# First pair of expert units written out ahead of the loop, its up product before two of the shared expert's down products

## The chip, the core and the metric

The kernel runs on one core of a Trainium2 chip. The metric is device microseconds for one call, the median of several runs. A profiled execution gives one trace beside them. TensorE (PE) does matrix products and transposes, VectorE (DVE) and ScalarE (ACT) do arithmetic and copies, GpSimd (POOL) issues the gathers of token rows, and SyncE (SP) issues nearly all other transfers. All engines run on their own and meet at semaphores.

## What is computed

One layer of a hybrid backbone over 384 tokens (128 of context, 256 latent): token mixers (gated linear attention and latent attention), then a mixture of experts. The part that the change touches is the last:

```python
def moe(h, lp):
    ...
    _, top_e = lax.top_k(jnp.where(e_mask, sel, -jnp.inf), TOP_K)   # 8 of 64 experts for a token
    ...
        a = jax.nn.silu(jnp.einsum('td,edf->tef', tb, lp['w_exp_gate'])) * jnp.einsum('td,edf->tef', tb, lp['w_exp_up'])
        a = a * gb[:, :, None].astype(a.dtype)
        return jnp.einsum('tef,efd->td', a, lp['w_exp_down'])
    ...
    shared = (jax.nn.silu(t @ lp['w_sh_gate']) * (t @ lp['w_sh_up'])) @ lp['w_sh_down']
    return (routed + shared).reshape(b_, l_, d)
```

Model width is 1024, each of the 64 experts has a hidden width of 256, all in float32. The three matrices of an expert are 1.05 MB each, 201 MB for all 64.

## The kernel before, in words

Ahead of the experts the kernel runs the token mixers, the router and the shared expert. The shared expert has three steps for each tile `t` of 128 tokens: `shared_up(t)`, `shared_turn(t)` (transposes of its activations) and `shared_down(t)`, two groups of four matmuls into the PSUM banks 0 and 1 (`hbank`), each taken to `acc` by ACT in `shared_out(t)`.

Experts are then handled in units of two, 128 token slots to a unit, and units in pairs, `half` 0 and 1. A pair `p` on PE (`pair`, L1055) is, in this order: `up(p, 0)`, 64 matmuls of the gathered tokens `xs` with the gate and up weights `raw_gu` of the unit into bank 0; `scatter` of the unit before (its output `ys` times the 0/1 matrix `place`, into banks 4 to 7, added to `acc` by DVE), three of six parts; `turn`, the transposes of the gated activations; the other three parts of the scatter; `gate_slots`, the gates and rows of the next pair's slots; `down(p, 0)`, 32 matmuls with `raw_dn` into banks 1 and 2; then the same for half 1, with `tokens_t`, the transposes of the next pair's gathered tokens, in place of the slots. ACT does `silu`, `take_turned`, `high_y` and half of `tokens`; DVE does `gated`, `add_scattered`, `gate_slots`, `places`, `low_y`, `picks` and the other half of `tokens`. POOL gathers the token rows `xg` of pair p+1 with two indirect DMAs when the slots are there and the old tokens have been transposed.

The weights of a unit are six loads of 1.05 MB, four for `raw_gu[half]`, two for `raw_dn[half]`. There are two sets of buffers, for half 0 and half 1, so the sync queue issues the loads of units 0 and 1 ahead of the loop and those of unit u+2 in a loop: `raw_gu[half]` when `up_done` shows that the up product of unit u is through, then `raw_dn[half]` when `y_done` shows the same for the down product. These waits stand in one queue in the order of the code.

The first pair runs through the same loop as the others (`Fori(0, ...)`). A unit before unit 0 does not exist. Its scatter is done all the same, with zeros: DVE clears `place` (L1822) and `ys` (L1866), and PE multiplies and DVE adds six tiles of zeros in the first pass. All three `shared_down` stand ahead of the loop, two before the tables of the overflow units (`overR`, `overJ`, `overK`), the third after them (L1041). Before its loop each engine loads two numbers of pairs, `n_pairs` and `final`, into registers. In this case there are 16 pairs, 7 of them wide.

Of the kernel before, what the change touches and what calls it, by code (L numbers as in the profile page):

```python
# [12 lines left out]
F32 = mybir.dt.float32  # L13
# [7 lines left out]
P = 128  # L21
D = 1024
NC = D // P
NT = 3
# [13 lines left out]
QPU = P // QTR  # L38
PAIR = 2 * P
# [78 lines left out]
def build(nc, A, O):  # L118

    ctx = ExitStack()  # L120
    with ctx:
# [175 lines left out]
        def rtile(*shape):  # L297
# [6 lines left out]
            if len(shape) == 3:  # L304
# [28 lines left out]
                 "score_ready mask_ready cnt_sb ownm_ready owner_ready jobs_ready tables_ready sh_sil_ready sh_a_ready "  # L333
                 "begun weight_ready h21_taken x1_half sq_half xm_ready h2_out row_ready row_taken xt_done next_ready shared_done zeroed gt2_in scaled_sb high_sb low_sb z_ready y_ready y_out "
                 "pick_ready gtmp_ready xs_act xs_dve gates_done slots_done place_ready up_done silu_done gated "
# [36 lines left out]

        def hbank(n, w=512):
            return ps[:, hr_no[n] % 2, 0:w]

# [146 lines left out]
        def _(pe):  # L522
            def mm(out, l, r, first, last):
                return nc.tensor.matmul(out, l, r, start=first, stop=last)  # L524
# [372 lines left out]

            def gate_slots(first):

                for k in range(2):  # L900
                    for t in range(NT):
                        g = gmov[:, t, first + k, :] if isinstance(first, int) else gmov[:, t, bass.ds(first + k, 1), :].rearrange("p a b -> p (a b)")
                        last = mm(ps[:, 2 if isinstance(first, int) else 3, PAIR + k * GCOL:PAIR + (k + 1) * GCOL], pick[:, t, k * P:(k + 1) * P], g, t == 0, t == NT - 1)
                last.then_inc(S["gates_done"], 1)
# [40 lines left out]
            pe.wait_ge(S["pick_ready"], 1)  # L945
            gate_slots(0)
            shared_turn(1)
            shared_turn(2)
            shared_down(0)
            shared_down(1)  # L950
            pe.wait_ge(S["owner_ready"], 1)
# [88 lines left out]

            shared_down(2)  # L1041
            pe.wait_ge(S["tables_ready"], 1)
            pe.wait_ge(S["wo_sb"], len(wo))
            pe.wait_ge(S["misc_sb"], len(misc))
            pe.sem_inc(S["turned"], 1)
            pe.sem_inc(S["y_done"], 2)
            for half in range(2):
                pe.wait_ge(xg_in[half], 16)
                for n in range(2):
                    tokens_t(half, n)  # L1050
            pe.wait_ge(S["hr_sb"], len(hr))
            n_pairs = pe.value_load(jobs[0:1, NJOB:NJOB + 1], min_val=NMAIN // 2, max_val=NUNIT // 2)
            final = pe.value_load(jobs[0:1, NJOB + 1:NJOB + 2], min_val=NMAIN // 2 - 1, max_val=NUNIT // 2 - 1)
# [22 lines left out]

            with pe.Fori(0, WIDE // 2) as p:
                pair(p, True)
# [25 lines left out]
        def _(act):  # L1104
# [148 lines left out]
            shared_out(0)  # L1253
            shared_out(1)
            shared_out(2)

# [24 lines left out]

            act.wait_ge(S["shared_done"], 1)
            act.sem_inc(S["ast_ready"], 1)
            tokens(0, 0)
            tokens(0, 1)
            n_pairs = act.value_load(jobs[0:1, NJOB:NJOB + 1], min_val=NMAIN // 2, max_val=NUNIT // 2)
            final = act.value_load(jobs[0:1, NJOB + 1:NJOB + 2], min_val=NMAIN // 2 - 1, max_val=NUNIT // 2 - 1)

            with act.Fori(0, final) as p:
                silu(p, 0)  # L1290
                take_turned(p, 0)
                high_y(p, 0)
                silu(p, 1)
                take_turned(p, 1)
                act.wait_ge(S["up_done"], 2 * p + 2)
                tokens(p + 1, 0)
                tokens(p + 1, 1)
                high_y(p, 1)
# [10 lines left out]
        def _(dve):  # L1309
# [462 lines left out]
            def picks(p):  # L1772
                cols_ = posq[:, :, bass.ds(p * 2 * QPU, 2 * QPU)] if not isinstance(p, int) else posq[:, :, 0:2 * QPU]
                V.tensor_tensor(pick[:].rearrange("p t (j s) -> p t j s", s=QTR),
                                slotrow.rearrange("p (j s) -> p j s", s=QTR).unsqueeze(1).to_broadcast([P, NT, 2 * QPU, QTR]),
                                cols_.unsqueeze(3).to_broadcast([P, NT, 2 * QPU, QTR]), ALU.is_equal).then_inc(S["pick_ready"], 1)

            def gate_slots(p):

                dve.wait_ge(S["gates_done"], p + 1)  # L1780
                o = ps[:, 2 if isinstance(p, int) else 3, PAIR:PAIR + 2 * GCOL].rearrange("p (k g) -> p k g", k=2)
                V.tensor_scalar(slot_row[:].unsqueeze(2), o[:, :, 2 * QPU:2 * QPU + 1], -1.0, float(TOK), ALU.mult, ALU.add).then_inc(S["row_ready"], 1)  # L1782
                V.tensor_copy(next_slots[:, 0:2].unsqueeze(2), o[:, :, 2 * QPU:2 * QPU + 1])
                V.tensor_tensor(gtmp, o[:, :, 0:2 * QPU], mine.unsqueeze(1).to_broadcast([P, 2, 2 * QPU]), ALU.mult).then_inc(S["gtmp_ready"], 1)
                dve.wait_ge(S["gtmp_ready"], p + 1)
                V.tensor_reduce(next_slots[:, 2:4], gtmp, AX.X, ALU.add).then_inc(S["next_ready"], 1)

            dve.wait_ge(S["misc_sb"], misc_no["tabK"] + 1)
            picks(0)
            gate_slots(0)  # L1790
            shared_act(2)
# [29 lines left out]

            V.memset(place[:].bitcast(F32), 0.0).then_inc(S["zeroed"], 1)  # L1822

# [5 lines left out]
            def places(k):  # L1829
                V.tensor_scalar(place[:, k, :], token, gtok[:, k:k + 1], None, ALU.is_equal).then_inc(S["place_ready"], 1)  # L1830
# [30 lines left out]
            take_slots(0)  # L1861
            dve.wait_ge(S["zeroed"], 1)
            dve.sem_inc(S["place_ready"], 1)
            places(0)
            dve.wait_ge(S["hr_done"], len(hr))
            V.memset(ys[:].bitcast(F32), 0.0).then_inc(S["zeroed"], 1)  # L1866
            dve.wait_ge(S["zeroed"], 2)
            dve.sem_inc(S["yl_done"], 2)
            dve.wait_ge(S["hr_sb"], len(hr))
            n_pairs = dve.value_load(jobs[0:1, NJOB:NJOB + 1], min_val=NMAIN // 2, max_val=NUNIT // 2)  # L1870
            final = dve.value_load(jobs[0:1, NJOB + 1:NJOB + 2], min_val=NMAIN // 2 - 1, max_val=NUNIT // 2 - 1)
# [25 lines left out]

            with dve.Fori(0, final) as p:
                dve.wait_ge(S["gates_done"], p + 1)
                picks(p + 1)  # L1900
                gated(p, 0)
                add_scattered(p, 0)
                gate_slots(p + 1)
                places(1)
                low_y(p, 0)
                gated(p, 1)
                add_scattered(p, 1)
                dve.wait_ge(S["up_done"], 2 * p + 2)
                tokens(p + 1, 0)
                tokens(p + 1, 1)  # L1910
                take_slots(p + 1)
                places(0)
                low_y(p, 1)
# [106 lines left out]
```

## Time and profile before

| | us |
|---|---|
| median of 3 runs | 791.27 (789.76 to 793.42) |
| the profiled execution | 791.03 |
| its span, from first to last instruction | 789.1 |
| PE busy in it | 746.7 (95%) |
| DVE busy | 392.7 (50%) |
| ACT busy | 133.7 (17%) |

Mean granted clock of TensorE is 0.998 of full speed. The page divides the span into 40 slices of 19.7 us each. The expert units begin at about 283 us, when the first matmul with `raw_gu` runs. The core moved 268.67 MB of data in the span, 340 GB/s on average.

In the rows below, a timeline row reads: start in us, duration in us, engine, line and operation, what it writes and reads, shapes, and how many instructions were merged into the row (such a row's duration runs from the start of the first to the end of the last). Brackets give idle time of the engine ahead of it and what ended that.

### The profile page before, as it was taken

Reading aid. Unit: us, or ns where it says so; the run is one execution under the profiler, and the core shown is the slowest. Engines: PE = TensorE matmul, PEld = TensorE weight load, DVE = VectorE, ACT = ScalarE, POOL = GpSimd, SP = SyncE. Lnnn points to the kernel's source line nnn. Section 1 sums busy time; section 2 is a strip of 40 time slices with the busy share of each in tenths; the row PEclk is TensorE's granted clock in tenths of the full one; section 3 lists DMA queues with packets and bytes.
Section 4 is the critical chain, followed back from the end, with each engine's and each line's share of the span. In section 5 each row is a group of like instructions: output and inputs, shape, how many; then the busy total and the mean of one; then the engine's idle time right before and its main releaser. Section 6 shows DMA issues by size and latency. Waiting matters only on the chain.

```text
span 789.1 us, 13795 instructions
## 1 busy us (share of the span) xinstructions
PE 746.7 (95%) x5071; PEld 361.3 (46%) x5071; DVE 392.7 (50%) x873; ACT 133.7 (17%) x285; POOL 43.1 (5%) x49
## 2 busy tenths in 40 slices
PE   4999998889999999999999999999999999999998
PEld 0554434475555554454454445444544453444433
DVE  2236369483686354364364345443543454435457
ACT  3124001310112112112112011111121111111110
POOL 0000001000000100101101101101011011010100
PEclk9999999999999999999999999999999999999999
DMA  9994466560702999999999999999999999999992
GB/s 339 385 385 144 172 230 233 206 211 1 276 28 81 381 387 422 419 422 419 421 421 420 421 420 420 422 419 420 421 421 421 420 420 421 419 420 422 420 405 85
DMA packets 49911, 268.67 MB, mean 340 GB/s; under 512 B 6300, under 2 KB 8732, under 8 KB 22752
## 3 DMA queue, kind: packets, MB, share of 16 engines
q1 hardware_dynamic: 45280, 255.77, 80.1%
q0 software_dynamic: 4608, 12.59, 4.1%
q8 instruction: 15, 0.25, 0.1%
q14 instruction: 8, 0.07, 0.0%
HBM read 269.01 MB, written 3.52 MB: 345 GB/s over the span
## 4 chain that ended last, share of the span: by engine, by line
PE 54%; DMA 33%; DVE 8%; SPq 2%; issue 2%; ACT 1%; DVEq 0%; ACTq 0%
PE ps L524 50%; DMA raw_gu<-in_w_exp_up 32%; DMA ada<-in_w_ada 1%; PE ps L972 1%; SPq L464 1%; SPq L465 1%; PE ps L831 0%; DVE probT L1537 0%; DVE small L1455 0%; DVE sq L1454 0%; DVE x L1620 0%; PE ps L598 0%; DVE xtmp L1618 0%; DVE h L1644 0%; DVE kend L1484 0%
## 5 line engine op out<-in xcount | busy, mean ns | idle before, releaser
L524 PE MATMUL ps<-raw_gu,xs 128*32 128x512 f32 x2048 | 226.1, 593 | 16.8 <-DMA raw_gu<-in_w_exp_up 15.9
L524 PEld LDWEIGHTS ps<-raw_gu,xs 128*32 128x32 f32 x2048 | 69.1, 110 | 171.5 <-issue 157.0
L524 PE MATMUL ps<-raw_dn,ast 128*32 128x512 f32 x1024 | 116.5, 595 | 0.0
L1856 DVE TENSOR_TENSOR acc<-acc,ps 128x512 f32<-128x512 f32 x186 | 113.6, 678 | 0.0
L1841 DVE SCALAR_TENSOR_TENSOR act_a<-ps,small,sil 128x256 f32<-128x256 f32 x32 | 15.5, 483 | 188.6 <-ACT sil L1261 188.6
L524 PE MATMUL ps<-ys,place 128*128 128x512 f32 x372 | 101.7, 410 | 0.0
L524 PEld LDWEIGHTS ps<-ys,place 128*128 128x128 f32 x372 | 65.4, 189 | 37.0 <-issue 26.0
L1849 DVE TENSOR_TENSOR ys<-ps,ys 128x512 fp32r<-128x512 f32 x60 | 41.5, 692 | 65.2 <-ACT ys L1274 65.2
L524 PEld LDWEIGHTS ps<-raw_dn,ast 128*32 128x32 f32 x1024 | 30.0, 109 | 60.2 <-issue 58.2
L1963 POOL DMA_INDIRECT xg<-h_spill,slot_row x32 | 31.9, 996 | 456.2 <-DVE slot_row L1782 451.3
L1274 ACT CAST ys<-ps 128x512 fp32r<-128x512 f32 x60 | 35.2, 586 | 113.0 <-PE ps L524 113.0
L1261 ACT ACTIVATE sil<-ps 128x256 f32<-128x256 f32 x32 | 12.3, 385 | 219.7 <-PE ps L524 219.7
L524 PE MATMUL ps<-w_out,mixedT 128*128 128x512 f32 x96 | 42.8, 595 | 1.1 <-issue 1.1
L972 PE MATMUL ps<-keep,xg 128*128 128x128 f32 x256 | 36.0, 288 | 0.0
L972 PEld LDWEIGHTS ps<-keep,xg 128*128 128x128 f32 x256 | 33.7, 194 | 3.9 <-issue 0.5
L524 PEld LDWEIGHTS ps<-w_out,mixedT 128*128 128x128 f32 x96 | 17.6, 190 | 20.6 <-issue 20.4
L1834 DVE COPY xs<-ps 128x512 f32<-128x512 f32 x32 | 22.0, 686 | 5.4 <-PE ps L972 5.4
L1279 ACT COPY xs<-ps 128x512 f32<-128x512 f32 x32 | 18.8, 587 | 28.2 <-PE ps L972 28.2
L524 PE MATMUL ps<-ada,small 128*2 128x256 f32 x128 | 11.4, 465 | 11.7 <-DMA ada<-in_w_ada 11.7
L524 PE MATMUL ps<-w_shgu,h2T 128*128 128x512 f32 x48 | 21.8, 598 | 0.0
L524 PE MATMUL ps<-hT,w_qk 128*128 128x384 f32 x64 | 21.8, 491 | 0.0
L524 PE MATMUL ps<-w_g,hT 128*128 128x512 f32 x48 | 21.4, 599 | 0.0
(300 smaller groups left out, 639.0 us busy)
## 6 DMA issues: line engine op xcount, KB each, us to landing
raw_gu<-in_w_exp_gate SPq DMA_DIRECT2D x64, 1024.0 KB, 16.4
raw_gu<-in_w_exp_up SPq DMA_DIRECT2D x64, 1024.0 KB, 18.5
raw_dn<-in_w_exp_down SPq DMA_DIRECT2D x64, 1024.0 KB, 18.7
ada<-in_w_ada SPq DMA_DIRECT2D x16, 512.0 KB, 11.3
ada2a<-in_w_ada SPq DMA_DIRECT2D x8, 1024.0 KB, 5.1
ada2b<-in_w_ada SPq DMA_DIRECT2D x8, 1024.0 KB, 6.3
w_out<-in_w_out SPq DMA_DIRECT2D x1, 4096.0 KB, 12.1
w_qk<-in_w_in SPq DMA_DIRECT2D x2, 1024.0 KB, 13.6
```

Of the source, the lines that this page charges most:

```text
L464: sp.dma_start(raw_gu[half][j][:, 0], gate_of(e)).then_inc(gu_in[half], 16)
L465: sp.dma_start(raw_gu[half][j][:, 1], up_of(e)).then_inc(gu_in[half], 16)
L524: return nc.tensor.matmul(out, l, r, start=first, stop=last)
L972: last = nc.tensor.transpose(ps[:, 4 + 2 * half + n, c * P:(c + 1) * P], xg[:, half, 4 * n + c::NC], ident)
L1261: nc.scalar.activation(sil[:], ps[:, 0, 0:DE], ACT.Silu).then_inc(S["silu_done"], 1)
L1274: nc.scalar.copy(ys[:, 0, n * 512:(n + 1) * 512], ps[:, 1 + n, :]).then_inc(S["yh_done"], 1)
L1279: nc.scalar.copy(xs[:, 0:4, half * P:(half + 1) * P], ps[:, 4 + 2 * half, :].rearrange("p (c s) -> p c s", c=4))\
L1834: V.tensor_copy(xs[:, 4:8, half * P:(half + 1) * P], ps[:, 5 + 2 * half, :].rearrange("p (c s) -> p c s", c=4))\
L1841: V.scalar_tensor_tensor(act_a[:], ps[:, 0, DE:2 * DE], gslot[:, half:half + 1], sil[:], ALU.mult, ALU.mult)\
L1849: V.tensor_tensor(ys[:, 1, h], ps[:, 1 + n, :], ys[:].bitcast(F32)[:, 0, h], ALU.subtract).then_inc(S["yl_done"], 1)
L1856: V.tensor_tensor(a, a, ps[:, 4 + (6 * half + k) % 4, :], ALU.add).then_inc(S["acc_done"], 1)
L1963: G.indirect_dma_start(xg[:, half], None, h2_dram, bass.IndirectOffsetOnAxis(ap=slot_row[:, half:half + 1], axis=0), bounds_check=TOK - 1, ...
```

## The change

The loops of PE, ACT and DVE begin at pair 1, and pair 0 is written out by hand. In it

- the scatter of the missing unit, its additions and both memsets are left out; the semaphores it would have raised are raised by hand;
- `up(0, 0)` comes before `shared_down(1)` and `shared_down(2)`, which take the place of that scatter on PE; their results go to banks 1 and 2, and ACT takes them between `silu(0, 0)`, `take_turned(0, 0)` and `high_y(0, 0)`;
- the tokens' transposes wait for the last overflow table's copy as before, but ACT's copies of them do not wait for the shared results any more;
- the wait for the tables and the loads of the two numbers of pairs come after pair 0.

```diff
         def hbank(n, w=512):
+            if n[0:3] in ("sd1", "sd2"):
+                return ps[:, 1 + int(n[3]), 0:w]
             return ps[:, hr_no[n] % 2, 0:w]
...
             shared_down(0)
-            shared_down(1)
             pe.wait_ge(S["owner_ready"], 1)
...
-            shared_down(2)
-            pe.wait_ge(S["tables_ready"], 1)
             pe.wait_ge(S["wo_sb"], len(wo))
             pe.wait_ge(S["misc_sb"], len(misc))
             pe.sem_inc(S["turned"], 1)
             pe.sem_inc(S["y_done"], 2)
+            pe.sem_inc(S["scat_done"], 6)
             for half in range(2):
                 pe.wait_ge(xg_in[half], 16)
                 for n in range(2):
                     tokens_t(half, n)
+            pe.wait_ge(S["hr_sb"], hr_no["sd01"] + 1)
+            pe.wait_ge(S["next_ready"], 1)
+            up(0, 0, True)
+            shared_down(1)
+            turn(0, 0, True)
+            shared_down(2)
+            pe.wait_ge(S["pick_ready"], 2)
+            pe.wait_ge(S["ast_ready"], 2)
+            gate_slots(2)
             pe.wait_ge(S["hr_sb"], len(hr))
+            down(0, 0, True)
+            up(0, 1, True)
+            scatter(0, 1, range(3))
+            turn(0, 1, True)
+            scatter(0, 1, range(3, 6))
+            for half in range(2):
+                pe.wait_ge(xg_in[half], 32)
+                for n in range(2):
+                    pe.wait_ge(S["acc_done"], 9 + 2 * half + n)
+                    tokens_t(half, n)
+            down(0, 1, True)
+            pe.wait_ge(S["tables_ready"], 1)
             n_pairs = pe.value_load(jobs[0:1, NJOB:NJOB + 1], min_val=NMAIN // 2, max_val=NUNIT // 2)
...
-            with pe.Fori(0, WIDE // 2) as p:
+            with pe.Fori(1, WIDE // 2) as p:
                 pair(p, True)
...
             shared_out(0)
-            shared_out(1)
-            shared_out(2)
...
-            act.wait_ge(S["shared_done"], 1)
             act.sem_inc(S["ast_ready"], 1)
             tokens(0, 0)
             tokens(0, 1)
+            silu(0, 0)
+            shared_out(1)
+            take_turned(0, 0)
+            shared_out(2)
+            high_y(0, 0)
+            silu(0, 1)
+            take_turned(0, 1)
+            act.wait_ge(S["up_done"], 2)
+            tokens(1, 0)
+            tokens(1, 1)
+            high_y(0, 1)
+            act.wait_ge(S["shared_done"], 1)
...
-            V.memset(place[:].bitcast(F32), 0.0).then_inc(S["zeroed"], 1)
...
             take_slots(0)
-            dve.wait_ge(S["zeroed"], 1)
             dve.sem_inc(S["place_ready"], 1)
             places(0)
-            dve.wait_ge(S["hr_done"], len(hr))
-            V.memset(ys[:].bitcast(F32), 0.0).then_inc(S["zeroed"], 1)
-            dve.wait_ge(S["zeroed"], 2)
             dve.sem_inc(S["yl_done"], 2)
+            dve.sem_inc(S["acc_done"], 6)
+            dve.wait_ge(S["gates_done"], 1)
+            picks(1)
+            gated(0, 0)
+            gate_slots(1)
+            places(1)
+            low_y(0, 0)
+            gated(0, 1)
             dve.wait_ge(S["hr_sb"], len(hr))
+            add_scattered(0, 1)
+            dve.wait_ge(S["up_done"], 2)
+            tokens(1, 0)
+            tokens(1, 1)
+            take_slots(1)
+            places(0)
+            low_y(0, 1)
...
-            with dve.Fori(0, final) as p:
+            with dve.Fori(1, final) as p:
```

Queues of SP and POOL are unchanged.

## Rows read from the trace of the kernel before

**Rows 1.** The page: GB/s in 40 slices; the gathers' queue (packets, MB, share).

```profile
GB/s 339 385 385 144 172 230 233 206 211 1 276 28 81 381 387 422 419 422 419 421 421 420 421 420 420 422 419 420 421 421 421 420 420 421 419 420 422 420 405 85
...
q0 software_dynamic: 4608, 12.59, 4.1%
```

**Rows 2.** Stretches: from:to, length, five engines' busy us, granted clock, DMA share, GB/s.

```profile
290.00:291.00 1.00, 1.00 (x5) 0.81 (x6) 0.57 (x2) 0.39 (x1) 0.00 (x0) 1.00 0.20 82
291.00:292.00 1.00, 1.00 (x7) 0.87 (x6) 1.00 (x2) 0.08 (x1) 0.00 (x0) 1.00 1.03 164
292.00:293.00 1.00, 1.00 (x6) 0.81 (x5) 1.00 (x3) 0.29 (x1) 0.00 (x0) 1.00 0.82 344
293.00:424.00 131.00, 131.00 (x1072) 58.95 (x1070) 60.65 (x122) 21.31 (x42) 9.90 (x10) 1.00 1.01 421
```

**Rows 3.** PE's timeline, one row; PE's waits for gate/up loads (total, times, longest).

```profile
434.49 7.07 PE L524 MATMUL ps<-raw_gu,xs 128*32 128x512 f32 x64 [1.55 <-DMA raw_gu<-in_w_exp_up]
...
PE ps L524 <- DMA raw_gu<-in_w_exp_up: 15.9, 22, 1.7
```

**Rows 4.** Timeline of the sync queue: first of four gate/up loads, and down loads.

```profile
290.15 0.33 SPq L464 DMA_DIRECT2D raw_gu<-in_w_exp_gate  x1
...
297.38 0.84 SPq L469 DMA_DIRECT2D raw_dn<-in_w_exp_down  x2
304.40 0.33 SPq L464 DMA_DIRECT2D raw_gu<-in_w_exp_gate  x1
...
320.14 0.34 SPq L464 DMA_DIRECT2D raw_gu<-in_w_exp_gate  x1
```

**Rows 5.** PE's timeline around the first pair.

```profile
267.06 7.03 PE L524 MATMUL ps<-w_shd,sh_aT 128*128 128x512 f32 x16
274.02 0.26 PE L524 MATMUL ps<-rt,late 64*1 64x56 f32 x2
...
276.42 3.70 PE L524 MATMUL ps<-w_shd,sh_aT 128*128 128x512 f32 x8
279.96 1.95 PE L972 MATMUL ps<-keep,xg 128*128 128x128 f32 x16
282.88 7.07 PE L524 MATMUL ps<-raw_gu,xs 128*32 128x512 f32 x64 [0.97 <-ACT xs L1279]
289.88 1.69 PE L524 MATMUL ps<-ys,place 128*128 128x512 f32 x6
...
293.68 3.64 PE L524 MATMUL ps<-raw_dn,ast 128*32 128x512 f32 x32
...
312.89 7.05 PE L524 MATMUL ps<-raw_gu,xs 128*32 128x512 f32 x64
```

**Rows 6.** DVE's timeline: last table, memset of ys, first instruction in the loop.

```profile
277.30 0.51 DVE L1766 TENSOR_TENSOR gmov<-ps,gmov 128x336 fp32r<-128x336 f32 x1
...
283.69 1.76 DVE L1866 MEMSET ys<- 128x2048 f32 x1 [0.37 <-issue]
287.46 0.96 DVE L1774 TENSOR_TENSOR pick<-keep,posq 128x768 fp32r<-128x768 f32 x1 [2.01 <-issue]
```

**Rows 7.** POOL's timeline: two gathers; then the tile's landing times, one each.

```profile
266.86 1.20 POOL L1963 DMA_INDIRECT xg<-h_spill,slot_row  x1 [20.11 <-DVE slot_row L1782]
268.36 0.99 POOL L1963 DMA_INDIRECT xg<-h_spill,slot_row  x1 [0.30 <-issue]
...
DMA to landing us min/median/max: 8.8/8.8/8.8
...
DMA to landing us min/median/max: 10.9/10.9/10.9
```

**Rows 8.** PE's timeline after an idle gap; two stretches, columns as in rows 2.

```profile
134.95 1.06 PE L693 MATMUL ps<-keep,key 128*96 128x128 f32 x4 [2.38 <-DVE keyT L1503]
...
10.50:11.50 1.00, 0.99 (x8) 0.11 (x8) 0.00 (x0) 1.00 (x2) 0.00 (x0) 1.00 1.06 406
...
135.50:138.00 2.50, 2.50 (x14) 2.36 (x13) 2.33 (x5) 0.00 (x0) 0.00 (x0) 0.50 0.47 200
```

More of the change, by code:

```diff
@@ L333, in build @@
                  "score_ready mask_ready cnt_sb ownm_ready owner_ready jobs_ready tables_ready sh_sil_ready sh_a_ready "
-                 "begun weight_ready h21_taken x1_half sq_half xm_ready h2_out row_ready row_taken xt_done next_ready shared_done zeroed gt2_in scaled_sb high_sb low_sb z_ready y_ready y_out "
+                 "begun weight_ready h21_taken x1_half sq_half xm_ready h2_out row_ready row_taken xt_done next_ready shared_done gt2_in scaled_sb high_sb low_sb z_ready y_ready y_out "
                  "pick_ready gtmp_ready xs_act xs_dve gates_done slots_done place_ready up_done silu_done gated "
@@ L896, in _, with gate_slots @@
             shared_up(1, range(6))
-            def gate_slots(first):
+            def gate_slots(first, bank=3):
                 for k in range(2):
@@ L902, in gate_slots @@
                         g = gmov[:, t, first + k, :] if isinstance(first, int) else gmov[:, t, bass.ds(first + k, 1), :].rearrange("p a b -> p (a b)")
-                        last = mm(ps[:, 2 if isinstance(first, int) else 3, PAIR + k * GCOL:PAIR + (k + 1) * GCOL], pick[:, t, k * P:(k + 1) * P], g, t == 0, t == NT - 1)
+                        last = mm(ps[:, bank, PAIR + k * GCOL:PAIR + (k + 1) * GCOL], pick[:, t, k * P:(k + 1) * P], g, t == 0, t == NT - 1)
                 last.then_inc(S["gates_done"], 1)
@@ L945, in _ @@
             pe.wait_ge(S["pick_ready"], 1)
-            gate_slots(0)
+            gate_slots(0, 2)
             shared_turn(1)
@@ L1285, in _ @@
             tokens(0, 1)
+            silu(0, 0)
[10 more added lines that the diff above has]
+            act.wait_ge(S["shared_done"], 1)
             n_pairs = act.value_load(jobs[0:1, NJOB:NJOB + 1], min_val=NMAIN // 2, max_val=NUNIT // 2)
             final = act.value_load(jobs[0:1, NJOB + 1:NJOB + 2], min_val=NMAIN // 2 - 1, max_val=NUNIT // 2 - 1)
-            with act.Fori(0, final) as p:
+            with act.Fori(1, final) as p:
                 silu(p, 0)
@@ L1772, in picks @@
             def picks(p):
-                cols_ = posq[:, :, bass.ds(p * 2 * QPU, 2 * QPU)] if not isinstance(p, int) else posq[:, :, 0:2 * QPU]
+                cols_ = posq[:, :, bass.ds(p * 2 * QPU, 2 * QPU)] if not isinstance(p, int) else posq[:, :, p * 2 * QPU:(p + 1) * 2 * QPU]
                 V.tensor_tensor(pick[:].rearrange("p t (j s) -> p t j s", s=QTR),
@@ L1776, in picks, with gate_slots @@
                                 cols_.unsqueeze(3).to_broadcast([P, NT, 2 * QPU, QTR]), ALU.is_equal).then_inc(S["pick_ready"], 1)
-            def gate_slots(p):
+            def gate_slots(p, bank=3):
                 dve.wait_ge(S["gates_done"], p + 1)
-                o = ps[:, 2 if isinstance(p, int) else 3, PAIR:PAIR + 2 * GCOL].rearrange("p (k g) -> p k g", k=2)
+                o = ps[:, bank, PAIR:PAIR + 2 * GCOL].rearrange("p (k g) -> p k g", k=2)
                 V.tensor_scalar(slot_row[:].unsqueeze(2), o[:, :, 2 * QPU:2 * QPU + 1], -1.0, float(TOK), ALU.mult, ALU.add).then_inc(S["row_ready"], 1)
@@ L1789, in _ @@
             picks(0)
-            gate_slots(0)
+            gate_slots(0, 2)
             shared_act(2)
```

## The prediction

> **What bounds the kernel now.** I read the page first, for the whole span, then stretches of it. From the fourteenth slice of the 40 on, where the experts' weights begin to stream, the row of GB/s reads 381 to 422 in every slice but the last [rows 1]. TensorE (PE) is at 9 tenths there as well, so the page alone doesn't say which of the two sets the end. The stretches do. From 293 to 424 us the DMA share is 1.01 at 421 GB/s and PE has no idle time either [rows 2]. From 434.49 us on the PE timeline and the list of waits show the change of hands: each product of a unit with its gate and up weights begins with idle time that a weight load ends, 22 times, 15.9 us together, 1.7 at most [rows 3]. So the end is set by the stream of weights: its 30 last units, six loads of 1.05 MB each, with the gathers between, run without a hole up to the tail. PE is faster than the stream in the wide pairs (30.0 us from 282.88 to 312.89 [rows 5]) and catches it up at about 430 us; until then PE's lateness costs nothing unless it leaves the stream without a request.
>
> There is one hole. Between 290 and 293 us the stream moves 82, 164 and 344 GB/s in the three microseconds [rows 2]. Against 421 that is 673 GB/s x us, or **1.6 us** of lost transfer. It is there because the sync queue (SP) had issued all that fits the buffers by 270, the last of it was through at about 290.2 by the flow, and the next load needs the buffer that the first up product frees: SP issued it at 290.15 [rows 4], and full flow was back 2.1 us later, which with the trickle in between counts as 1.65 us from issue to effective flow. That hole is all the change can win by its main idea, 0.2% of the time; less than 0.5% can't be told from no change in a measurement of this kernel.
>
> **Part by part.** I follow up(0,0), the gate-and-up product of unit 0, through the new order. Each later request of SP hangs on PE: gate/up loads on the end of an up product, down loads on a down product.
>
> *Order ahead of up(0,0).* Sixteen matmuls of two shared down products took 267.06 to 274.02, so one takes 3.48 us; the overflow tables took 274.02 to 276.42, the third product 3.54, and the sixteen transposes of gathered tokens began at 279.96 [rows 5]. With one product gone from ahead of the tables and one from behind them PE finishes the tables at 267.06 + 3.48 + 2.40 = 272.9. It can't go on, for two reasons. VectorE (DVE) must have taken the last table, in before at 277.81 [rows 6], 3.48 earlier now: 274.3. And the tokens must have come: the two gathers were issued at 266.86 and 268.36 and landed 8.8 and 10.9 us after that, at 275.7 and 279.3 [rows 7]. Nothing in the change moves them. In before the products of the shared expert covered this wait; now nothing does. Transposes of the second half can't begin before 279.3 and take 1.0 us (half of 1.95 [rows 5]); the copies of the first half lie in the gap. So up(0,0) starts at 280.4 instead of 282.88: 2.5 us earlier, not 7. The 0.97 us of idle time ahead of it in before [rows 5], a pair of register loads and the loop's entry, moves to the end of pair 0.
>
> *Removed scatter and memsets.* Scatter of the missing unit is two groups of six matmuls, the first 1.69 us long at 289.88 [rows 5], 1.6 each from start to start: 3.2 us of PE go. DVE loses two memsets, the longer of 1.76 us [rows 6], and six additions; DVE wasn't waited for here, so they are worth nothing. Copies of tokens before the shared results are free too: ScalarE (ACT) reaches them in time either way.
>
> *Moved in.* Two shared down products, 2 x 3.48 = 7.0 us, now stand between up(0,0) and down(0,0), where the scatter stood. ACT's silu and DVE's gating, 0.9 us, hide under the first, the copy of the turned activations under the second. ACT copies four banks more in this stretch (0.59 us each), each behind a product that PE follows with another; the last must be done before down(0,0): about 0.2 us of wait, after the slot product of 0.7 us has covered the rest.
>
> *Sum for PE.* up(0,0) 280.4 to 287.4; products and turn 7.2 us to 294.6; slots 0.7; wait 0.2; down(0,0) starts at 295.5 instead of 293.68. From there the old distances hold. SP's issues [rows 4]: first gate/up load 290.15 becomes 287.67 (-2.5); first down load 297.38 becomes 299.2 (+1.8); second gate/up load 304.40 becomes 306.2 (+1.8); that of pair 1, 320.14, becomes 322.0 and with the loop's entry of 0.97, now uncovered, 322.9 (+2.8). The entry isn't shown at its new place: 0 if queued matmuls cover it, 2.01 as DVE's idle time ahead of its first instruction in the loop [rows 6]; I take 0.97, PE's own row. The gathers of pair 1 move with PE's slot product, 1.8 us later too, and land ahead of the transposes that need them by as much as before. Pool's and SP's loops are as they were; the tables they wait for come 3.5 us earlier and were no limit.
>
> *The stream.* A unit is 6.29 MB at 421 GB/s: 14.94 us; two gathers add 0.79 MB (12.59 MB in 32 [rows 1]), 1.9 us. Before: effective restart at 291.8; unit 2 and gathers to 308.6 (next request effective at 306.05, no hole); unit 3 to 323.55 (next effective at 321.8, no hole, **1.75 us to spare**). After: no hole at 290.2; unit 2 and gathers to 307.0, but the next request is effective at 306.2 + 1.65 = 307.9: hole 0.9. Unit 3 to 322.8; next effective at 322.9 + 1.65 = 324.6: hole 1.8. That makes 2.7 us of hole against 1.6: **+1.05 us**. Later requests have room again, since the stream (31.8 us a pair) falls 1.8 us a pair behind PE. More than half of what the first request wins is lost with the next one, and the rest and more with the third.
>
> *Clock.* PE now idles about 2.8 us, works 1, idles 2.6, and works 1 before up(0,0). The nearest row is at 132.6 to 134.9: after 2.38 us of idle time the granted clock was 0.50, its level of 1.2 GHz, from 135 to 138.5, and four transposes took 1.06 us, where sixteen take 1.95 here [rows 5, 8]. By it the clock is halved from about 276 on and for some 3.5 us of work from 279.3: transposes +0.85, the first part of up(0,0) +0.85, together +1.7 us on PE. Against it: after 10.5 us of idle time at the very start the rows show 1.00 [rows 8]. Bounds 0 and 1.75. I take 1.7, as the row with dense work ahead of the gap is the nearer. The second gate/up request is then effective at 309.6 and the third at 326.3, and everything is 1.7 later still: **+2.75 us**.
>
> The Trainium skill (TensorE: Matmul & The Clock Gate, Part 1) says that the array falls to half rate when it has been idle and is let go again by sustained work, and advises against gaps between bursts. By that rule the dip comes, and the sum is +2.75; without it, +1.05. The row at 135 agrees with it, that at the start doesn't.
>
> **Rivals.**
> - *No dip.* All else as above: +1.05. For it: two short gaps rather than a single one, and work of 1 us between; the row at the start. Against: the row at 135.
> - *The hole closes and none opens.* The tokens land 2.6 us or more before 279.3, or PE's hand-written pair has fewer waits than I count; then all requests come in time and the stream wins the full 1.6 us. It needs up(0,0) at or before 277.8. For it: the tables' order lets PE be there at 276.4. Against: the landing times, which hang on DVE's slots at 265.9 and on a queue shared with the weights, both unchanged.
> - *PE's chain in pair 0 is longer than I count* (slower than before). After the third request each microsecond of it is one of the total. The loop's entry at 2.01 rather than 0.97, and the two hand-overs between shared products and ACT's copies (0.59 + 0.1 each, uncovered), add 1.04 + 1.4 to the dip: +5.2. It decides from 1.2 us more than my sum on. For it: no row shows ACT with copies ahead of the turn. Against: each copy has 3.5 us of PE work to hide under.
> - *The change does not do what it says*: tokens land so late that up(0,0) starts no earlier than 282.88. Then PE is 2.5 us later again: +3.5 to +5.2.
>
> **How the numbers follow.** The profiled execution took 791.03 us with a span of 789.1; the median of the three timed runs is 791.27 (789.76 to 793.42), so the sum on it is good to some 0.3. Likeliest: dip, 791.03 + 2.75 = **793.8**, chance 0.47, own range 792.6 to 795.3. No dip: 792.1, chance 0.23. Holes close: 789.4, 0.13. Longer chain: 796.2, 0.13. Doesn't do it: 794.5 to 796.2, 0.04. Limits of 0.5% are 787.3 and 795.2. No case reaches the lower: faster 0.02. Slower: the longer chain 0.12, the last case 0.02, the upper edge of the likeliest 0.04, together 0.18. Same: 0.80. The range from 789.8 to 796.0 leaves out half of the closing case and half of the longer chain, with a little at the edges, under 0.2.
>
> **What the profile of the changed kernel would show.** No hole near 290; SP's first gate/up reload near 287.7 to 289.4; PE with idle time of 2 to 3 us twice between 273 and 279; the next reloads at 306 to 308 and 323 to 325; two smaller holes near 308 and 324; the granted clock at half somewhere between 276 and 283; from 435 on the same waits for weights as now, shifted by the total difference. If the transposes of the second half run before 278, the gather step is wrong; if the clock stays at 1.00, the dip is; if a hole appears later than 330, the stream's spare time is.

## The result, and the profile after

| | before | changed |
|---|---|---|
| median, us | 791.57 (6 runs, 789.76 to 793.42) | 796.92 (6 runs, 795.30 to 800.09) |
| profiled execution, us | 791.03 | 795.55 |
| its span, us | 789.1 | 793.7 |
| mean granted clock | 0.998 | 0.991 |

The ratio is 1.0069, with a 95% interval from 1.0058 to 1.0081: the change costs 4.6 to 6.4 us. Slower was the side I gave 0.18; the range ended at 796.0, below the median. The two profiled executions lie 4.5 us apart. Of all executions in this document one, the profiled one of the experiment e6, took 1280.8 us at a mean granted clock of 0.561; it stands in no comparison.

The part of the kernel ahead of the experts takes a different time from one execution to the next, so stretches are compared from one mark: the start of the last of the shared expert's turns (`shared_turn(2)`), at 266.71 us in before (just ahead of the 267.06 of [rows 5]) and 267.18 after, and between 266.17 and 270.16 in all profiles below. From it to the end before takes 522.4 us and the changed kernel 526.5.

First, PE's timeline of the changed kernel, the answer to [rows 5]:

```profile
267.18 0.51 PE L858 MATMUL ps<-keep,sh_a 128*128 128x128 f32 x2 [0.63 <-DVEq L1759]
267.52 3.60 PE L526 MATMUL ps<-w_shd,sh_aT 128*128 128x512 f32 x8
...
276.63 1.97 PE L973 MATMUL ps<-keep,xg 128*128 128x128 f32 x8 [3.11 <-DMA xg<-h_spill,slot_row]
280.24 1.97 PE L973 MATMUL ps<-keep,xg 128*128 128x128 f32 x8 [1.64 <-DMA xg<-h_spill,slot_row]
282.14 8.91 PE L526 MATMUL ps<-raw_gu,xs 128*32 128x512 f32 x64
290.98 3.70 PE L526 MATMUL ps<-w_shd,sh_aT 128*128 128x512 f32 x8
...
294.75 3.60 PE L526 MATMUL ps<-w_shd,sh_aT 128*128 128x512 f32 x8
297.78 1.13 PE L526 MATMUL ps<-gmov,pick 128*128 128x10 f32 x6
299.02 3.64 PE L526 MATMUL ps<-raw_dn,ast 128*32 128x512 f32 x32
```

Two gaps end with the landing of the gathered tokens, 3.11 and 1.64 us. After each, eight transposes take 1.97 us where sixteen took 1.95 in before, and the up product lasts 8.91 us instead of 7.07. Then the stretches of the same kernel (columns as in [rows 2]), which answer to [rows 2, 8]:

```profile
275.50:286.00 10.50, 7.73 (x36) 4.13 (x40) 2.75 (x5) 1.17 (x2) 0.00 (x0) 0.51 1.02 425
...
290.00:291.00 1.00, 1.00 (x13) 0.14 (x5) 0.00 (x0) 0.00 (x0) 0.00 (x0) 1.00 0.28 115
291.00:292.00 1.00, 1.00 (x7) 0.52 (x4) 0.45 (x1) 0.38 (x1) 0.00 (x0) 1.00 0.08 33
292.00:293.00 1.00, 1.00 (x4) 0.52 (x3) 0.03 (x1) 0.00 (x0) 0.00 (x0) 1.00 0.81 197
293.00:294.00 1.00, 1.00 (x3) 0.38 (x2) 0.00 (x0) 0.59 (x1) 0.00 (x0) 1.00 0.75 303
302.00:306.00 4.00, 4.00 (x44) 1.26 (x40) 1.07 (x2) 0.59 (x1) 0.24 (x1) 1.00 0.99 346
310.00:312.00 2.00, 2.00 (x11) 1.67 (x10) 1.99 (x4) 0.37 (x1) 0.00 (x0) 1.00 0.62 184
326.00:328.00 2.00, 2.00 (x11) 1.67 (x10) 2.00 (x5) 0.37 (x1) 0.00 (x0) 1.00 0.74 221
```

The granted clock is 0.51 on average for 10.5 us, where 0.50 is its level of 1.2 GHz, and the weight stream has four weak places where before had one: near 290, 304, 311 and 327. The sync queue shows what opens each of them, the answer to [rows 4]:

```profile
291.27 0.33 SPq L466 DMA_DIRECT2D raw_gu<-in_w_exp_gate  x1
...
302.72 0.81 SPq L471 DMA_DIRECT2D raw_dn<-in_w_exp_down  x2
309.74 0.33 SPq L466 DMA_DIRECT2D raw_gu<-in_w_exp_gate  x1
...
325.49 0.34 SPq L466 DMA_DIRECT2D raw_gu<-in_w_exp_gate  x1
```

Counted from the mark, the first reload is issued at 24.1 us (23.4 before), the first down load at 35.5 (30.7), the second reload at 42.6 (37.7), the third at 58.3 (53.4): none is earlier, three are 4.9 us later.

To put a number on the stream I take the 84 stretches of 1 us from 2 to 86 us after the mark and add up (421 - GB/s) / 421. This **lost transfer** is 1.6 us in before and 5.65 in the changed kernel, where the four weak places hold about 2.4, 0.7, 1.1 and 1.2 us of it: the hole near 290, which the change was to close, is larger than before. From about 435 us on both kernels are alike: 22 products of the changed kernel begin with a short wait for weights, 15.1 us together, as many as in [rows 3]. Two of them:

```profile
439.03 7.07 PE L526 MATMUL ps<-raw_gu,xs 128*32 128x512 f32 x64 [0.76 <-DMA raw_gu<-in_w_exp_up]
...
770.91 7.07 PE L526 MATMUL ps<-raw_gu,xs 128*32 128x512 f32 x64 [0.84 <-DMA raw_gu<-in_w_exp_up]
```

### The profile page after: what moved, and what is told of

Same layout as the page of the kernel before. It is cut to its first block, busy times and chain, and to the rows that moved or that the text cites. A ratio compares the mean times of both kernels' runs of the same rounds, so it can differ in the third digit from the quotient of the medians.

```text
span 793.7 us, 13708 instructions
## 1 busy us (share of the span) xinstructions
PE 747.9 (94%) x5059; PEld 359.6 (45%) x5059; DVE 386.9 (49%) x865; ACT 133.7 (17%) x285; POOL 43.0 (5%) x49
## 4 chain that ended last, share of the span: by engine, by line
PE 52%; DMA 35%; DVE 7%; SPq 2%; issue 2%; ACT 1%; POOL 0%; DVEq 0%; ACTq 0%; POOLq 0%
PE ps L526 49%; DMA raw_gu<-in_w_exp_up 32%; DMA xg<-h_spill,slot_row 1%; PE ps L973 1%; DMA ada<-in_w_ada 1%; SPq L466 1%; SPq L467 1%; PE ps L833 0%; DVE probT L1567 0%; DVE small L1485 0%; DVE sq L1484 0%; PE ps L600 0%; SPq L401 0%; DVE x L1650 0%; DVE xtmp L1648 0%
## 5 line engine op out<-in xcount | busy, mean ns | idle before, releaser
L526 PE MATMUL ps<-raw_gu,xs 128*32 128x512 f32 x2048 | 228.0, 597 | 15.1 <-DMA raw_gu<-in_w_exp_up 15.1
L1885 DVE TENSOR_TENSOR acc<-acc,ps 128x512 f32<-128x512 f32 x180 | 110.0, 681 | 0.0
L526 PE MATMUL ps<-ys,place 128*128 128x512 f32 x360 | 98.4, 409 | 0.0
L526 PEld LDWEIGHTS ps<-ys,place 128*128 128x128 f32 x360 | 63.3, 189 | 35.7 <-issue 25.1
L973 PE MATMUL ps<-keep,xg 128*128 128x128 f32 x256 | 37.9, 297 | 4.7 <-DMA xg<-h_spill,slot_row 4.7
L526 PE MATMUL ps<-ada,small 128*2 128x256 f32 x128 | 11.4, 465 | 12.0 <-DMA ada<-in_w_ada 12.0
## 6 DMA issues: line engine op xcount, KB each, us to landing
raw_gu<-in_w_exp_up SPq DMA_DIRECT2D x64, 1024.0 KB, 17.7
ada<-in_w_ada SPq DMA_DIRECT2D x16, 512.0 KB, 11.4
```

Source lines behind the costliest of these rows:

```text
L973: last = nc.tensor.transpose(ps[:, 4 + 2 * half + n, c * P:(c + 1) * P], xg[:, half, 4 * n + c::NC], ident)
L1885: V.tensor_tensor(a, a, ps[:, 4 + (6 * half + k) % 4, :], ALU.add).then_inc(S["acc_done"], 1)
```

## The experiments

Ratios are to the kernel before, which ran beside each kernel on the same chip, with their 95% interval; e1 to e4 ran on one chip, e5 to e12 on another, and the medians of before there were 791.48 and 791.77 to 792.05. "Third" is the issue of the third reload after the mark, "lost" the lost transfer, "end" the span's end after the mark, these three from each kernel's one profile. A filler is a matmul whose result is used nowhere.

| kernel | median | ratio | third | lost | end |
|---|---|---|---|---|---|
| before | 791.57 | 1 | 53.4 | 1.6 | 522.4 |
| changed | 796.92 | 1.0069 (1.0058 to 1.0081) | 58.3 | 5.65 | 526.5 |
| e1 changed, again | 797.54 | 1.0071 (1.0058 to 1.0084) | 58.3 | 6.8 | 527.0 |
| e2 11 fillers | 797.00 | 1.0066 (1.0054 to 1.0078) | 59.2 | 7.1 | 528.0 |
| e3 product 1 in the gap | 789.18 | 0.9967 (0.9955 to 0.9979) | 53.2 | 0.4 | 520.4 |
| e4 old order by hand | 789.88 | 0.9974 (0.9962 to 0.9986) | 53.2 | 1.2 | 521.5 |
| e5 5 fillers | 793.85 | 1.0028 (1.0016 to 1.0039) | 55.6 | 4.1 | 524.9 |
| e6 e3 + 1.7 us | 791.41 | 0.9998 (0.9985 to 1.0011) | | | |
| e7 e3 + 2.6 us | 794.27 | 1.0030 (1.0015 to 1.0044) | 55.4 | 3.3 | 524.8 |
| e8 e3 + 5.2 us | 795.64 | 1.0049 (1.0031 to 1.0066) | 58.1 | 5.2 | 526.3 |
| e9 gathers alone | 792.98 | 1.0024 (1.0012 to 1.0035) | 53.4 | 3.0 | 522.9 |
| e10 e3 + 0.9 us | 790.97 | 0.9991 (0.9978 to 1.0005) | 53.7 | 0.7 | 520.8 |
| e11 e6 again | 792.02 | 1.0005 (0.9996 to 1.0014) | 54.5 | 2.4 | 524.0 |
| e12 e3, gathers alone | 792.68 | 1.0011 (0.9999 to 1.0023) | 50.4 | 3.0 | 523.2 |

End minus lost lies between 519.9 and 521.6 in all thirteen profiles, while lost runs from 0.4 to 7.1, and a straight line through them gives 1.08 us of the end for each microsecond lost. So a microsecond of stream that is lost in this stretch is about a microsecond of the end, whatever made it.

**e1** is the changed kernel unedited.

> The changed kernel once more, for use beside the other three on one chip. Again 4.6 to 6.4 us over the kernel before; granted clock at half for some 10 us around 276 to 286; holes in the weight stream near 290, 310 and 326.

It came out the same, and its timeline too: gaps of 2.65 and 2.17 us, an up product of 8.85 us. Its lost transfer is 6.8 us against 5.65, so one profile gives that number to 1 us or so.

**e2 and e5: keep TensorE at work in its gaps.** This is e2; e5 has 3 and 2 in the place of 6 and 5.

```diff
+            def fill(n):
+                for _ in range(n):
+                    mm(ps[:, 3, :], ident, w_shd[:, 0, 0:512], True, True)
...
             pe.wait_ge(S["wo_sb"], len(wo))
+            fill(6)
             pe.wait_ge(S["misc_sb"], len(misc))
...
             for half in range(2):
+                fill(5 * half)
                 pe.wait_ge(xg_in[half], 16)
```

> The changed kernel with 11 matmuls into an unused bank (6 ahead of the wait for the last table, 5 between the token transposes of half 0 and half 1), so that TensorE works through its two gaps; their results are used nowhere. Theory A (the clock's fall costs TensorE 0.99 us in the second half's transposes and 1.84 in up(0,0), 2.8 together, and each is a microsecond of the end): clock stays 1.00, up(0,0) lasts 7.07 us, the first reload is issued near 288.0 rather than 291.3, the third 2.8 us earlier; the total falls by 2.8 us to some 2 to 3 over the kernel before. Rival B (the order in pair 0 alone is what costs, the clock falls for nothing): the third reload is where it was and the total falls by less than 1 us. Rival C (the landing of the tokens sets everything): the same as B for up(0,0)'s start, but up(0,0) shorter.

The clock stayed up, but a filler took 0.87 us rather than the 0.43 I had reckoned, so the eleven overran the gaps and up(0,0) began 17.7 us after the mark, 2.7 later than in the changed kernel. What the clock gave back the fillers took; e2 decides nothing, and e5 has fillers that fit.

> The changed kernel with 5 filler matmuls of 0.87 us (3 in the first gap, 2 in the second; their results are used nowhere), half of what e2 had, so that they fit the gaps of 3.1 and 2.6 us. Theory A (the halved clock costs PE 2.8 us in pair 0, and each goes to the end through the third reload): clock 1.00, up(0,0) 7.07 us long and begun some 1 us sooner, third reload at 55.5 us after the last shared turn instead of 58.3, the stream loses some 2.5 us less there: total 2.0 to 3.0 us below the changed kernel, 2.5 to 3.5 over the kernel before. Rival B (clock free, order costs): third reload where it was, total within 0.8 us of the changed kernel.

```profile
279.22 1.16 PE L973 MATMUL ps<-keep,xg 128*128 128x128 f32 x8 [1.07 <-DMA xg<-h_spill,slot_row]
280.31 7.08 PE L526 MATMUL ps<-raw_gu,xs 128*32 128x512 f32 x64
```

These two rows of e5's PE timeline have the full rate, and the third reload is at 55.6 instead of 58.3. The ratio is 1.0028 against 1.0069 and 1.0071, some 3.3 us below the changed kernel, a little more than forecast; by the profiles' ends, 524.9 against 526.5 and 527.0, it is 1.6 to 2.1 us. **The halved clock is between two fifths and three fifths of the loss.** Useless work makes the kernel faster. What is left, 2.2 us by the ratio, I put down to the order of the products, which e3 and e4 take up.

**e3: useful work in the gap.**

```diff
             pe.wait_ge(S["wo_sb"], len(wo))
+            pe.wait_ge(S["next_ready"], 1)
+            pe.wait_ge(S["hr_sb"], hr_no["sd01"] + 1)
+            shared_down(1)
             pe.wait_ge(S["misc_sb"], len(misc))
...
-            pe.wait_ge(S["hr_sb"], hr_no["sd01"] + 1)
-            pe.wait_ge(S["next_ready"], 1)
             up(0, 0, True)
-            shared_down(1)
-            turn(0, 0, True)
             shared_down(2)
+            turn(0, 0, True)
...
             shared_out(0)
+            shared_out(1)
...
             silu(0, 0)
-            shared_out(1)
+            shared_out(2, (0,))
             take_turned(0, 0)
-            shared_out(2)
+            shared_out(2, (1,))
```

The second argument of `shared_out` names the halves to copy.

> The changed kernel with the shared product 1 in the first gap (ahead of the token transposes) instead of behind up(0,0), its copies ahead of the tokens' copies on ScalarE, and the shared product 2 between up(0,0) and the turn. Theory A (PE's gaps and the 7 us put between up(0,0) and down(0,0) are the cost, pair 0 by hand as such is free): up(0,0) starts near 281, ends near 288, down(0,0) starts near 293, third reload at or before 319.5; no hole from 290 on; total 1.6 us below the kernel before (its whole hole), so 5.5 to 7 below the changed one. Rival B (the pair written by hand costs at the loop's entry or in the fetch of code): 1 us or more above the kernel before although the reloads come early.

```profile
274.62 3.70 PE L526 MATMUL ps<-w_shd,sh_aT 128*128 128x512 f32 x8
278.15 1.05 PE L973 MATMUL ps<-keep,xg 128*128 128x128 f32 x8
281.55 1.16 PE L973 MATMUL ps<-keep,xg 128*128 128x128 f32 x8 [2.34 <-DMA xg<-h_spill,slot_row]
282.64 7.07 PE L526 MATMUL ps<-raw_gu,xs 128*32 128x512 f32 x64
289.64 3.70 PE L526 MATMUL ps<-w_shd,sh_aT 128*128 128x512 f32 x8
```

In e3's PE timeline the product fills the first gap, the second one (2.34 us, with that product and 1 us of transposes ahead) doesn't drop the clock, and the up product has its 7.07 us. Its mark is at 268.34, so up(0,0) starts 14.3 us after it, against 16.2 in before and 15.0 in the changed kernel. Only 0.4 us of the stream is lost. At 789.18 us and 0.9967 it is faster than both kernels. Against before that is 2.6 us (1.7 to 3.6), where its profile ends 2.0 us earlier and 1.2 us less is lost; against the changed kernel it is 8.1 us by the ratios and 6.2 by the ends, where I had allowed 5.5 to 7. Rival B falls: writing the pair by hand costs nothing that shows.

**e4: by hand, old order.**

```diff
             shared_down(0)
+            shared_down(1)
             pe.wait_ge(S["owner_ready"], 1)
...
+            shared_down(2)
             pe.wait_ge(S["wo_sb"], len(wo))
...
-            pe.wait_ge(S["hr_sb"], hr_no["sd01"] + 1)
+            pe.wait_ge(S["hr_sb"], len(hr))
             pe.wait_ge(S["next_ready"], 1)
             up(0, 0, True)
-            shared_down(1)
             turn(0, 0, True)
-            shared_down(2)
```

The results of the products go to banks 0 and 1 again, and ACT takes them ahead of the tokens, as in before.

> Pair 0 written out by hand without the missing unit's scatter, as in the changed kernel, but all three shared products where the kernel before has them, ahead of up(0,0). One part of the change alone. Theory A: up(0,0) starts near 282 (no register loads ahead of it), ends near 289; PE waits 1.5 us for the gated activations ahead of the turn, which nothing covers now; down(0,0) starts near 292.5; reloads at 289.3, 303, 319: the total is 0.5 to 1.2 us below the kernel before. Rival B (by-hand code as such costs): 1 us or more above it. Rival C (the uncovered 1.5 us drop the clock): half clock near 290, and 1 to 3 us above.

0.9974: with the pair by hand and the missing unit's scatter left out, but the products where they were, the kernel gains 1.1 to 3.0 us by the interval; the profile's end is 0.9 us earlier. Theory A's 0.5 to 1.2 us is at the lower edge of that. Of rival C the dip came and the slower kernel did not. PE waited 1.02 us for the gated activations and 0.55 for their copy, and after these two small gaps down(0,0) took 5.34 us instead of 3.64:

```profile
293.38 0.50 PE L999 MATMUL ps<-keep,act_a 128*128 128x128 f32 x2 [1.02 <-DVE act_a L1868]
294.44 0.80 PE L524 MATMUL ps<-gmov,pick 128*128 128x10 f32 x6 [0.55 <-ACT ast L1286]
295.18 5.34 PE L524 MATMUL ps<-raw_dn,ast 128*32 128x512 f32 x32
```

The granted clock is 0.89 on average from 285 to 300. But the third reload still came at 53.2 us after the mark, and the dip cost the end nothing that the total shows. So of the change's two ideas the one helps and the other does the harm: between e4 and the changed kernel, which differ in the place of two products of 3.5 us and of their copies, lies 0.95% of the time.

**e6, e7, e8, e10, e11: PE's lateness in doses.** The edit to e3 is one line, with n of 2, 3, 6, 1 and 2 and `fill` as in e2:

```diff
             up(0, 0, True)
             shared_down(2)
+            fill(n)
             turn(0, 0, True)
```

> e3 (pair 0 by hand, shared product 1 in the gap) with 2 filler matmuls, 1.74 us of PE work that is used nowhere, between the shared product 2 and the turn: only PE's lateness in pair 0 is dosed, the first reload and the clock stay as in e3. Theory A (a late reload costs only what goes beyond the stream's spare time, 0.8 us by the ledger): e3 + 0.9 us. Rival B (the stream slows before it runs dry): e3 + 1.5 to 2.5 us.

> The same with 3 filler matmuls, 2.6 us. Theory A: e3 + 1.8 us. Rival B: e3 + 2.5 to 3.5 us, at or above the kernel before.

> The same with 6 filler matmuls, 5.2 us, PE's lateness at the third reload then about that of the changed kernel, with full clock and the first reload in time. Theory A: e3 + 4.4 us, 2 over the kernel before. Rival B: e3 + 5.5 to 7.5 us, so 3 to 5 over the kernel before, as the changed kernel has it: PE's lateness in pair 0 alone explains that kernel. Rival C (a late first reload is what costs): e3 + 3 or less.

> e3 with 1 filler matmul of 0.87 us between the shared product 2 and the turn (its result is used nowhere). Third reload 54.1 us after the last shared turn. Theory A (0.8 us to spare): e3 within 0.3 us, the stream loses 0.4 to 0.6 us between 20 and 86 us after that turn. Theory B (the stream thins out before it is empty): e3 + 0.8 to 1.8 us, 1.0 to 2.2 us lost.

> The kernel of e6 once more, to have its profile: third reload 54.9 us after the last shared turn. Theory A: 1.3 us lost in the same stretch. Theory B: 2 to 3 us lost; total e3 + 2 to 3 us, as e6's median was.

e6 has no profile to set beside the others; e11 is the same kernel. The lost transfer is 0.4 us without a dose, then 0.7, 2.4, 3.3 and 5.2 with 0.9, 1.7, 2.6 and 5.2 us, by which the third reload is 0.5, 1.3, 2.2 and 4.9 us later than in e3. From that lateness theory A (0.8 us to spare, then one for one) would have 0.4, 0.9, 1.8 and 4.5, so the measured loss is 0.3, 1.5, 1.5 and 0.7 us above it. The same shows in all seven profiles whose third reload comes 54.5 us after the mark or later: third minus lost lies between 51.5 and 52.9, and theory A asks for 53.6. So each loses more than theory A allows, as theory B says. How much more, 0.7 to 2.1 us, is no sharper than two profiles of one kernel differ (5.65 and 6.8).

The medians say the same more roughly: by the ratios e3 + 1.9 us, 2.5 and 3.0 (e6, e11), 5.0 and 6.5. All of these lie 1.0 to 2.1 us above what the profiles lose more than e3's. Set against the kernel before instead, the two accounts meet within 0.7 us: by the ratios -0.7, +0.4 (e11), +2.4 and +3.9 us, by the loss -0.8, +0.8, +1.7 and +3.7. So it is e3 that stands out, with -2.6 by its ratio and -1.2 by its loss. It ran on the other chip and was not run again there, and totals counted from it may be 1 to 1.5 us too high.

Rival C falls: with the first reload in time and the full clock, e8 is 3.9 us over the kernel before. PE's lateness from the turn on accounts for most of the changed kernel's 5.5 us. A dose moves the down load, the second and the third reload together, so no run shows which of them counts most; in e8, 3.0 of the 5.2 us are lost at the down load's place, 33 to 38 us after the mark.

Where does theory B's microsecond come from? These are stretches of e8, whose down loads were issued at 302.23:

```profile
300.00:301.00 1.00, 1.00 (x16) 0.26 (x8) 0.00 (x0) 0.42 (x1) 0.69 (x2) 1.00 0.24 98
301.00:302.00 1.00, 1.00 (x14) 0.27 (x10) 0.69 (x1) 0.16 (x1) 0.94 (x1) 1.00 0.69 90
302.00:303.00 1.00, 1.00 (x16) 0.38 (x12) 0.14 (x1) 0.58 (x1) 0.00 (x0) 1.00 0.81 295
303.00:304.00 1.00, 1.00 (x16) 0.26 (x8) 0.55 (x1) 0.00 (x0) 0.00 (x0) 1.00 0.94 135
```

Between the end of the gate/up loads and the first bytes of the down loads, from 301 to 304, little but the gathers is left, and the engines are 69 to 94% busy at 90 to 295 GB/s. The changed kernel has the same place at 302 to 306, with weights still flowing for part of it: share 0.99, 346 GB/s. The profile's view of its queues, for 302 to 307, gives the gathers 47.4% of the engines' time for 0.76 MB; in before, in the same stretch, it is 22.4% for 0.43 MB. These are the changed kernel's:

```profile
q1 hardware_dynamic: 142, 1.03, 50.8%
q0 software_dynamic: 288, 0.76, 47.4%
```

So a second request, the down load, was late as well, and the gathers that I had let cover for it don't carry a full stream. That much is seen in the rows; that it is theory B's microsecond is argued, as no run dosed the down load by itself.

**e9 and e12: gathers ahead of the weights.**

```diff
             sp.wait_ge(S["begun"], 1)
+            for half in range(2):
+                sp.wait_ge(xg_in[half], 16)
             load_gu(1, second)
```

> The changed kernel, but the sync queue waits for both gathers of pair 0 to land before it issues the four gate/up loads of unit 1 and the two down loads. Theory A (the gathers land 9.3 and 11.4 us after their issue because they share the engines with 6 MB of weights queued with them): they land within 6 to 8 us, PE's gaps shrink to 1 us or less each, the clock stays at 1.00 and up(0,0) starts at least 2 us earlier; the weight loads issued later may open a hole of up to 2 us near 275. Rival B (the landing time is the gather's own): they land as before, unit 1's loads come 8 us late, and the total is 3 us or more over the changed kernel.

The landing times were 8.1 and 7.4 us instead of 9.3 and 11.4: without unit 1's loads in the queue the second gather lands 4 us sooner, the first 1.2. The transposes ran together, up(0,0) began 11.6 us after the mark, 3.4 earlier than in the changed kernel. The clock fell all the same, after a gap of 1.93 us with the 2.4 us of table matmuls, 64 rows each, ahead of it:

```profile
273.00:274.00 1.00, 0.00 (x0) 0.00 (x0) 0.79 (x2) 0.00 (x0) 0.00 (x0) 1.00 1.00 398
274.00:275.00 1.00, 0.55 (x4) 0.55 (x5) 0.00 (x0) 0.00 (x0) 0.00 (x0) 0.96 0.21 78
275.00:276.00 1.00, 1.00 (x7) 1.00 (x6) 0.00 (x0) 0.58 (x1) 0.00 (x0) 0.50 0.00 0
```

The same rows show the price, a hole in the stream at 274 to 277. Lost transfer is 3.0 us, all of it there; no reload leaves a hole afterwards. That trade, 3.0 for 5.65, takes 3.6 us off the changed kernel (1.0024), a kernel faster by a hole put where none was. My expectation of a steady clock missed.

> e3 with the sync queue's wait of e9. If the gathers land earlier, PE's gap of 2.3 us between the two halves' transposes goes and all reloads come earlier by up to 2 us; but e3 loses only 0.4 us of the stream after the start, so at most that can be won, and a hole near 275 costs up to 2: total between e3 - 0.4 and e3 + 2 us.

In e3 there is nothing to trade for: every reload came 2.6 to 2.8 us earlier, and still 3.0 us are lost instead of 0.4. It is 1.0011 against 0.9967, 3.5 us slower by the ratios, more than the 2 I allowed, and 2.8 by the profiles' ends.

## Why the prediction was wrong, point by point

- **What bounds the kernel, and the hole.** Right. End minus lost transfer is the same within 1.7 us in all profiles, and e3 won the hole and lost none elsewhere. The remark that less than 0.5% can't be told from no change was too cautious: the interval here is 0.12% to either side.
- **Order ahead of up(0,0).** Right in kind: PE waits for both gathers and the gaps stand where I put them. The landings came 0.5 us later than in before's profile (9.3 and 11.4 us for 8.8 and 10.9), within what executions differ: e1's gaps are 0.5 shorter and 0.5 longer.
- **Clock.** Right in kind, wrong in size: the sum had 3.5 us of work at half rate, until about 282.8, and 1.7 us of cost. The half rate lasted from 275.6 to 285.9, 10.3 us with 7.6 of work in them, and cost 2.8 us (second transposes +1.0, up product +1.8). I had taken the length from the one gap of [rows 8], with work right after it that no gap broke; here a second gap followed, and the clock rose only after 3.7 us of the up product. I had also called the work ahead of that gap dense; it was 1.5 us of transposes behind 2 us of narrow matmuls (128*2). "No dip" falls, and with it the row of the kernel's first matmuls as a guide. These are PE's rows in before, ahead of the gap:

```profile
129.23 1.04 PE L524 MATMUL ps<-ada2a,small 128*2 128x512 f32 x8
130.08 1.04 PE L524 MATMUL ps<-ada2b,small 128*2 128x512 f32 x8
131.06 1.51 PE L693 MATMUL ps<-keep,key 128*96 128x128 f32 x12
```

- **Moved in.** Right: from up(0,0)'s end to the start of down(0,0) I had 8.1 us (287.4 to 295.5) and it took 8.0 (290.98 to 299.02).
- **The loop's entry.** Wrong: 0.97 in the sum, 0.0 measured. Second to third reload is 15.75 us, and 15.74 in before. Behind 32 queued matmuls it costs PE nothing. Ahead of the first pair it was idle time: e4, which has the same order there without the entry, goes from the transposes to the up product with none. That too little was queued there to cover it is my reading and not shown.
- **PE's sum.** It came out close by luck, two errors of opposite sign: third reload late by 4.5 us (2.8 + 1.7) in the text, by 4.9 in the trace. The first reload however, which I had 0.8 us early with the dip (2.5 less 1.7), was 0.7 late, 1.1 of the 1.5 us by the clock and the rest by the landings. So the hole near 290 did not close, it grew.
- **The stream.** This is the step that failed most. 1.75 us to spare ahead of the third reload were to turn 4.5 us of lateness into 2.75. Measured: 4.9 us of lateness, and 4.1 us more lost than in before. The doses show 0.4 lost at the outset, 2.4 from 1.3 us of further lateness (third reload 53.2 and 54.5). The ledger counted only gate/up requests, and let the gathers' 1.9 us stand as full flow behind a down load that was late itself. It is the lost transfer near 304, and thinner flow on both sides of each hole, that it lacked; how the missing microsecond divides between them is open.
- **Rest.** 4.1 of lost transfer is 4.1 of the 4.1 us by which the ends differ from the mark on, and with 0.5 us by which the mark is later 4.6 of span. The medians differ by 5.35 (interval 4.6 to 6.4). The profiled executions of the changed kernel were among its fastest, 795.55 the second of six and e1's 795.64 the first of six; what made the others longer is open. So of the 3.1 us between the forecast 793.8 and the median 796.9 about 0.4 is PE, 1.0 the stream, 0.5 lies ahead of the mark, and the rest, some 1.3, is a median above the profiled execution.
- **Rivals.** "The chain is longer than I count" had the right outcome, 796.2, by luck: neither the entry nor the hand-overs to ScalarE cost anything. The likeliest case had the mechanism, and its size was off by the clock and by the stream together.

## What to carry to other kernels

When a stream of loads sets the end, work on another engine that is moved costs nothing until a reload becomes late, and then about a microsecond for each: list each reload of each kind, when its buffer comes free and how long the stream can run without it, small scattered gathers not counted as full flow. Work that looks removable ahead of a product may be what covers a transfer, and here also what kept TensorE's clock up; move it behind the wait that it covers only if something else stands in for it. Two changes made together should be taken apart: here, by the ratios, one was worth 0.26% and the other lost more than three times that.

## What the runs showed of the hardware

- TensorE's granted clock fell after gaps of 3.1 us (after), 2.65 (e1) and 1.93 us (e9) with 2.4 us of 64-row matmuls ahead, and after the 2.38 us of [rows 8] with transposes and narrow matmuls ahead. It did not fall after 2.34 us (e3), 2.30 (e8), 2.23 (e7) and 2.16 us (e10, e11), where 3.7 us of 128x512 products and 1 us of transposes stood ahead. In e4 it fell after two gaps of 1.02 and 0.55 us with two transposes between them. The Trainium skill (TensorE: Matmul & The Clock Gate, Part 1) tells of a clock that follows activity, and these rows agree: the length of the gap alone didn't decide. Gap and what surrounds it must be read together.
- Two indirect gathers of 0.4 MB each, with next to nothing beside them, had the DMA engines 69 to 94% busy at 90 to 295 GB/s (e8, 301 to 304), where weight loads of 1 MB flow at 421.
- A gather issued with the six loads of unit 1 in the queue landed 11.4 us after its issue (the changed kernel), without them 7.4 (e9); the one ahead of it 9.3 and 8.1.
